# Wide matmuls ordered tile by tile instead of column group by column group

## The reference, cut to what matters

```python
z = h @ w_in                                            # mixer of block 1
return y @ w_out
return (jax.nn.silu(h @ w_gate) * (h @ w_up)) @ w_down  # 2048 -> 5632 -> 2048
...
x = x + gt1 * (jnp.concatenate([o_mla, o_na, o_fn], axis=-1) @ w_out[l])
u = h @ w_up                                            # block 2, 2048 -> 2 x 5632
return (jax.nn.silu(gate) * val) @ w_down
```

## Time and profile before

| | before |
|---|---|
| time, median of 3 | 2372.5 us (2372.32 to 2372.93) |
| profiled execution, time | 2372.5 us |
| profiled execution, span | 2370.7 us |
| PE busy | 2360.1 us (100%) |
| DVE busy | 1775.0 us (75%) |
| ACT busy | 1161.2 us (49%) |
| PE in lines 1170 and 1178, share of the chain that ended last | 44% and 22% |

### The profile page before, as it was taken

The page is one execution under the profiler, slowest core; times in us unless marked ns, Lnnn a source line. Parts: engine busy times, 40 slices in busy tenths (PEclk is TensorE's granted clock), DMA queues, the critical chain, the costliest instruction groups (busy, mean ns, idle before and its releaser), DMA issues.

```text
span 2370.7 us, 42045 instructions
## 1 busy us (share of the span) xinstructions
PE 2360.1 (100%) x14820; PEld 2107.1 (89%) x14820; DVE 1775.0 (75%) x2859; ACT 1161.2 (49%) x1703; POOL 0.2 (0%) x4
## 2 busy tenths in 40 slices
PE   9999999999999999999999999999999999999998
PEld 9998899988888888889988988688888888888888
DVE  6676678899878888889887755467776577766775
ACT  6454446555545664445623343456444444444455
POOL 0000000000000000000000000000000000000000
PEclk9999999999999999999999999999999999999999
DMA  7775567688778886787567622054656555655654
GB/s 283 282 281 190 188 230 242 194 293 296 266 248 286 290 283 235 270 280 258 203 222 265 236 72 91 17 195 160 201 180 197 192 180 193 193 188 185 193 188 142
DMA packets 141880, 509.03 MB, mean 215 GB/s; under 512 B 15824, under 2 KB 17360, under 8 KB 141392
## 3 DMA queue, kind: packets, MB, share of 16 engines
q1 hardware_dynamic: 141776, 507.60, 63.5%
HBM read 505.44 MB, written 2.10 MB: 214 GB/s over the span
## 4 chain that ended last, share of the span: by engine, by line
PE 98%; DVE 1%; ACT 0%; DMA 0%; issue 0%; SPq 0%; ACTq 0%; DVEq 0%
PE ps L1170 44%; PE ps L1178 22%; PE ps L1212 8%; PE ps L1214 8%; PE ps L1213 8%; PE ps L1564 1%; PE ps L1238 1%; PE ps L1240 1%; PE ps L1239 1%; PE ps L1582 1%; PE ps L1384 1%; PE ps L1365 0%; PE ps L1573 0%; PE ps L1409 0%; PE ps L1390 0%; DMA raw<-in_stream 0%
## 5 line engine op out<-in xcount | busy, mean ns | idle before, releaser
L1765 DVE TENSOR_TENSOR lo<-raw,hi 128x1024 fp32r<-128x1024 f32 x753 | 914.5, 1222 | 400.6 <-ACT hi L596 398.4
L596 ACT ACTIVATE hi<-raw 128x1024 fp32r<-128x1024 f32 x753 | 794.9, 1060 | 764.1 <-PE ps L1178 451.6
L1170 PE MATMUL ps<-hs,hi 128*128 128x512 f32 x2880 | 886.9, 394 | 0.0
L1178 PEld LDWEIGHTS ps<-hs,lo 128*128 128x128 f32 x2880 | 529.2, 188 | 115.0
L1178 PE MATMUL ps<-hs,lo 128*128 128x256 f32 x2880 | 553.2, 279 | 0.0
L1170 PEld LDWEIGHTS ps<-hs,hi 128*128 128x128 f32 x2880 | 439.8, 188 | 7.7 <-issue 0.4
L1170 PE MATMUL ps<-hid,hi 128*128 128x512 f32 x1192 | 366.7, 393 | 0.0
L1178 PEld LDWEIGHTS ps<-hid,lo 128*128 128x128 f32 x1192 | 218.8, 188 | 47.5
L1790 DVE SCALAR_TENSOR_TENSOR wm<-wm,cbx 128x1024 f32<-128x1024 f32 x192 | 233.8, 1219 | 5.6 <-DMA wm<-in_mod_stream 5.6
L1178 PE MATMUL ps<-hid,lo 128*128 128x256 f32 x1192 | 228.7, 279 | 0.0
L1212 PE MATMUL ps<-xs,hi 128*128 128x258 f32 (+2 forms) x776 | 225.9, 291 | 0.4 <-DVE lo L1765 0.4
(11 more groups left out here) (341 smaller groups left out, 2765.6 us busy)
## 6 DMA issues: line engine op xcount, KB each, us to landing
raw<-in_stream SPq DMA_DIRECT2D x753, 512.0 KB, 4.2
wm<-in_mod_stream SPq DMA_DIRECT2D x192, 512.0 KB, 4.6
out_tokens<-y_final SPq DMA_DIRECT2D x4, 512.0 KB, 3.7
h<-in_tokens SPq DMA_DIRECT2D x3, 544.0 KB, 8.9
cx<-in_ctx_tokens SPq DMA_DIRECT2D x6, 256.0 KB, 5.8
cbx<-in_c_rows SPq DMA_DIRECT2D x1, 1024.0 KB, 7.8
cbc<-in_c_rows SPq DMA_DIRECT2D x1, 1024.0 KB, 6.1
na<-in_na_bias SPq DMA_DIRECT2D x1, 1024.0 KB, 4.8
```

The costliest lines, as they stand in the source:

```text
L596: act.activation(hi[:, slot, :], raw[:, slot, :], ACT.Copy).then_inc(hi_done, 1)
L1170: last = pe.matmul(ps[:, bank, :].rearrange("p (a n) -> p a n", a=2), hi[:, slot, w], xs(kt)[0], start=kt == 0, stop=kt == last_k)
L1178: last = pe.matmul(ps[:, bank, 0:NX], lo[:, slot, w], xs(kt)[1], start=False, stop=False)
L1765: dve.tensor_tensor(lo[:, slot, :], raw[:, slot, :], hi[:, slot, :].bitcast(F32), ALU.subtract)\
```

## The change

In `wide_chunk` the loop over tiles goes outside. Tile 0 runs through its four kt with hi and lo in turn, then tile 1 does. The wait for a bank moves to just before its own tile; the waits for tokens are made in tile 0's pass. At the last kt of a half lo still comes before hi. The matmuls, their operands and their number are the same, and `chunk_used` is still counted by the last one of the chunk.

```diff
-                if j == 0:
-                    for t in range(ly.tiles):
+                for t in range(ly.tiles):
+                    bank = (2 * hf + t) % 4
+                    if j == 0:
+
                         pe.wait_ge(bank_free, ly.tbase + 2 * hf + t + 1 + it * ly.tpi)
                         if banks_ready is not None:
                             pe.wait_ge(*banks_ready(t))
-
-                def by_hi(kt, k):
-                    for t in range(ly.tiles):
-                        bank = (2 * hf + t) % 4
+                    both = ps[:, bank, :].rearrange("p (a n) -> p a n", a=2)
+                    for k in range(kk):
+                        kt = j * kk + k
+                        if x_ready is not None and t == 0:
+                            pe.wait_ge(*x_ready(kt))
                         w = slice(k * width + t * P, k * width + t * P + P)
-                        last = pe.matmul(ps[:, bank, :].rearrange("p (a n) -> p a n", a=2), hi[:, slot, w], xs(kt)[0],
-                                         start=kt == 0, stop=kt == last_k)
-                    return last
-
-                def by_lo(kt, k):
-                    for t in range(ly.tiles):
-                        bank = (2 * hf + t) % 4
-                        w = slice(k * width + t * P, k * width + t * P + P)
-                        last = pe.matmul(ps[:, bank, 0:NX], lo[:, slot, w], xs(kt)[1], start=False, stop=False)
-                    return last
-
-                for k in range(kk):
-                    kt = j * kk + k
-                    if x_ready is not None:
-                        pe.wait_ge(*x_ready(kt))
-                    if kt == last_k:
-                        by_lo(kt, k)
-                        ins = by_hi(kt, k)
-                    else:
-                        by_hi(kt, k)
-                        ins = by_lo(kt, k)
+                        pair, x_hi = xs(kt)
+                        if kt == last_k:
+                            pe.matmul(ps[:, bank, 0:NX], lo[:, slot, w], x_hi, start=False, stop=False)
+                        ins = pe.matmul(both, hi[:, slot, w], pair, start=kt == 0, stop=kt == last_k)
+                        if kt != last_k:
+                            ins = pe.matmul(ps[:, bank, 0:NX], lo[:, slot, w], x_hi, start=False, stop=False)
                 ins.then_inc(chunk_used, 1)
```

## The result

The changed kernel is slower: 2399.22 us (2398.26 to 2402.1, 4 runs) against 2372.72 for the kernel before on the same chip, ratio 1.0115, 95% interval 1.0101 to 1.0130. That is 26.5 us. The forecast was no change, 2371.9 us; the time lies above the range of 2357 to 2393 us, where rival 2 had put it (2400 us).

The account below looks back on a forecast made before the run. PE's matmuls were taken to bound the kernel. From 2372.5 us, order 0, out_chunk -1.25 and up2s +0.65 gave -0.6 and a forecast of 2371.9 us; range 2357 to 2393 us, the forecast's own 2368.5 to 2375.

Parts of the forecast that it names:

- rival 2: Wide-layer pairs: alternation makes every matmul slow, 353 ns a pair, +28 us, 2400 us; chance 0.21 with its smaller versions.
- What bounds the kernel: Whole kernel: PE's matmuls set the time; 4472 hi/lo pairs at 346.7 ns make 1550 us, 65% of the span.
- No price on one bank: Wide-layer matmuls: staying in one bank makes no difference; one-bank streams give 693.0 ns a group against 693.4.
- The step that failed: Wide-layer pairs: alternating widths keep their stream prices, 346.7 ns a pair, no change, 3.1 us either way; chance 0.44.
- a lag of recorded starts: Single wide-layer matmuls: excess taken on after a wide one and given back after a narrow one; only the sum counts.
- The other reading: Single wide-layer matmuls: each cost is real and set by the predecessor alone; alternation gives 226 + 118, 344 ns.
- The formula that it weighed: Any warm matmul: columns over 2.4 GHz plus about 2.5 ns; a group costs 650 ns in either order, no change.
- Rival 1: Wide-layer pairs: the predecessor sets the cost, 344 ns a pair, -12.1 us, with the waits 2359.8 us; chance 0.26.
- Rival 3: Wide-layer pairs: both widths at their cheap values, 339 ns a pair, -34 us, 2338 us; chance 0.03.
- The waits: PE's waits: out_chunk(0) gains 1.25 us, the start of up2s loses 0.65 us, total -0.6 us.
- rival 4: Waits alone go wrong: out_chunk's gain is lost and token waits appear at layer starts, up to 2379 us; chance 0.06.
- The bands for the ends of halves: Distance of ends of halves in long loops: 11.09 us if unchanged; 11.01, 11.3 or 10.85 for the pair-price alternatives.

Follow-up runs that it names:

- e3: Changed kernel (tile outside), but two kt taken together within a tile, hi, hi, lo, lo (hi, lo, lo, hi at a half's end): 2375.84 us, ratio 1.0014.
- e8: Changed kernel, but each tile starts a half with two 512-column hi and two lo, then three 256-column matmuls per pair: 2345.43 us, ratio 0.9886.
- e1: Kernel before with its loop order and waits, but hi and lo of each tile alternating (hi t0, lo t0, hi t1, lo t1): 2404.97 us, ratio 1.0139.
- e2: Kernel before, but hi t0, lo t1, hi t1, lo t0, except at a half's first and last kt, which keep twos: 2403.08 us, ratio 1.0127.
- e6: Kernel before with two kt taken together, four hi in a row, then four lo: 2374.01 us, ratio 1.0006.
- e4: Kernel before with each 512-column matmul cut into two of 256, all widths equal: median 2366.86 us, ratio 0.9968, runs in two clusters.
- e9: e5 with one single 512-column matmul replacing two of 256 in tile 0 at kt 8 of each half: 2378.39 us, ratio 1.0019 to the kernel before.
- e7: e5 with two neighbours exchanged at each half's start, making the 512-column matmuls single (hi, lo, hi, lo): 2406.60 us, ratio 1.0141.
- e5: e4 with the first kt of each half as two 512-column hi, then two lo; all others three of 256: 2346.00 us, ratio 0.9889.

## Why the prediction was wrong

**What bounds the kernel** held: 4472 pairs, 65% of the span, and 1 ns per pair 4.5 us. The loss is 6.2 ns times that number.

**No price on one bank** held, and not only for equal widths: `e3` and `e8` run unequal widths in one bank at the old cost, while `e1` and `e2` leave the bank at every second step and are as slow as the changed kernel, which leaves it at every eighth.

**The step that failed** is the one on which the forecast rested: "the widths cost what they cost in streams of their own although here they change twice per group", so that "a pair costs 233.2 + 113.3 = 346.5 ns plus at most twice 0.2". The sum of 693.0 ns from the streams against 693.4 was right, and `e6` confirms it for fours. But it was carried to a sequence in which the 113.3 ns do not hold. They are no property of 256 columns; they are one of the two states of a stream, and 117.8 ns is the other (`e4`'s dear stretch). In twos every group leaves the cheap state behind it; a single wide matmul between narrow ones sets the dear one (`e9`, `e7`). In alternation every wide matmul is a single one: 235 + 118 = 353 ns.

Both signs had been in the trace of before. The 512 columns at 226 and at 235 and the 256 at 118 and 114 were read as a lag of recorded starts that only shifts cost between neighbours. The other reading, that a matmul behind a 512-column one costs more, did not fit the prediction's own stream of 512, where all stand behind one and cost 230 or 236 in turn. And a third sign stood in the groups by shape of the kernel before, in the stage `by_token`:

```profile
L1239 PE MATMUL ps<-hi,hs 128*128 128x256 f32 x128 | 35.8, 280 | 0.0
```

280 less 163 is 117, and the starts of that stage lie 117.8 ns apart on average: the dear value, in a stream of nothing but 256 columns. The prediction took its price of 256 columns from the cheap streams alone and didn't ask why equal instructions have two prices. The formula that it weighed, of the Trainium skill's page "TensorE: Matmul & The Clock Gate", section "Back-to-back issue gap", has one price for one width, and the section calls it the gap of an isolated matmul; the estimate from it for 256 columns is 109.2 ns. The traces don't agree with it: these streams have two prices above it, 113.3 and 117.8 ns.

**Rival 2** was right in size (28 us; 27.7 measured by the ends of halves) and in what each matmul would cost, "each hi would meet a lo of 118 ahead of it ... and would cost 235". It did not know of the two states, and of the two causes that it named, two equal widths or two banks in turn, the banks play no part. So what was held against it, that equal widths in one bank cost nothing, was no argument. Its chance was too small, and the range ended below it. **Rival 1**, prices by predecessor, falls with `e4`: 113 and 118 behind the same predecessor. **Rival 3**, both cheap values, fell with the result: no matmul of line 1178 in the stretch above is at 276.

**The waits** held in sign and size: 1.47 us from the transposes to the mix against 1.25 forecast, 0.65 lost at up2s as forecast. No new token waits appeared (**rival 4**): PE's idle time behind DVE in line 1176 is below 1 us in all.

**The bands for the ends of halves** had it: 11.3 us for rival 2, 11.29 measured.

## What to carry to other kernels

Before a price per instruction is taken from a stream, look at the minimum and the maximum of the same instruction in all of the trace: two sharp values with nothing between are two states, and the question is then which sequence sets which. In a PE-bound stream of two matmul widths like this one, put the wide ones in twos or more throughout, with none alone between narrow ones. Where a stream of narrow ones is free to fall into either state, start it with the sequence that sets the cheap one; a median over such runs describes neither.

## What the runs showed of the hardware

On fp32r matmuls with 128 x 128 weights, each with its own weight load, with the granted clock at 2.4 GHz:

- A long stream of 256 columns costs 113.3 or 117.8 ns each, 4% apart, and stays in its state for over 1500 matmuls, until foreign matmuls come between (`e4` at 703.8 and 885.2 us).
- Two of 512 and two of 256 cost 226, 235, 118 and 113 ns and leave the cheap state, whether in one bank or two, with the same or other tokens (before, `e3`). One of 512 costs 226 ns out of the cheap state and leaves the dear one (`e9`). Four of 512 and two of 256 behind an alternating stretch leave the dear one (`e2`).
- Three of 256 in the cheap state (340 ns) do the work of one of 512 and one of 256 (346.7 ns), although they load weights a third time; the wide form takes 1526.9 us in `e5` and 1552.9 before.
- Back-to-back matmuls into one bank cost what they cost with the bank changing each time: the wide form takes 1527.4 us in `e8` and 1526.9 in `e5`.
- Stages that no edit touched take part. In `out1`, line 1204 of `e1` against line 1202 of the changed kernel, the same instructions (duration ns min/median/max):

```profile
L1204 PE MATMUL ps<-ysc,lo x78: 281/281/281, 380.0 to 429.8; 128*128 128x256 f32 x78
```
```profile
L1202 PE MATMUL ps<-ysc,lo x78: 276/276/276, 379.9 to 427.9; 128*128 128x256 f32 x78
```

`dn1c` shows the same (281 against 276). Together the two stages have 1344 such matmuls, worth up to 6 us, more than the 4.7 us that the prediction took for the noise of a measurement. `out1` ends before the first matmul that any edit moved, and all eleven kernels have the same code up to there; in their traces it takes 89.4 us in five and 91.9 us in six. So there the state can't come from the edited order; for `dn1c`, which comes later, that isn't shown.

What the two states are physically, no run here shows. Line 1178's weight loads are recorded with up to 192 ns in `e4`'s dear stretch and with 187 or 188 in its cheap one, but in the changed kernel's dear stretch line 1178 has 187 or 188 too, so they are no general sign of the state. That the sequence sets the states is shown for the sequences above; why it does, and why `e2`'s end of a half is an exception, is open.
